# Modulation vectors by rows: GpSimd multiplies, ScalarE sums

## Chip, cores and metric

The kernel runs on one core of a Trainium2 chip. The metric is the device time of one execution in microseconds (us), as the median of several runs. A core has the engines TensorE (PE in the profile, its weight loads apart as PEld), VectorE (DVE), ScalarE (ACT), GpSimd (POOL) and SyncE (SP), which here only issues DMAs. Each runs its own list of instructions in order, and they meet by semaphores.

## What is computed

Two blocks of two layers each, on 256 tokens of width 1024, all in float32. Every layer derives shift, scale and gate, 3072 numbers, from a condition vector and a matrix of 1024 x 3072. The second block does it for two conditions (the tokens' and the context's).

```python
c_silu = jax.nn.silu(c)                                  # first block, one condition
mod = c_silu @ w_ada + b_ada
shift, scale, gate = jnp.split(mod, 3, axis=-1)
u = rms_norm(x, norm_g) * (1 + scale[:, None]) + shift[:, None]
z = u @ w_in                                             # then three attentions, gates, w_out
...
shift, scale, gate = jnp.split(jax.nn.silu(c) @ w_ada + b_ada, 3, axis=-1)       # second block
shift_c, scale_c, gate_c = jnp.split(jax.nn.silu(c_ctx) @ w_ada + b_ada, 3, axis=-1)
```

The rest of a layer is a wide projection, several attentions (one with a search for the top 64 keys of each query, one with a sliding window and sinks, one "stick-breaking"), gates and an output projection.

## The kernel before

The work is written as five scripts, one for each stage: prologue (the first modulation of layer 0), one0 and one1 (the two layers of the first block, one1 with the context's part of the second block's first layer), two0 and two1 (the second block). A script is a list of items such as ("proj", "cq", 0, (0,)) or ("logits", 3). Every engine walks the same list and emits its own instructions for each item, so the script sets the order on all five, and an engine that waits at an item holds up all of its later items.

Names of items: "proj" is a projection of 256 output columns, 16 products of 128x128 by 128x256 on TensorE and a copy out of PSUM on ScalarE (on VectorE for av, bv, cv). A job is one piece of attention: "logits" (TensorE, then a maximum on VectorE and exponentials on ScalarE), "soft" (VectorE scales them), "turn" (TensorE transposes, ScalarE copies), "mix" (TensorE by the values, VectorE copies). In stick-breaking jobs GpSimd masks in "soft" and "turn". weave() puts a projection between these steps so that TensorE has work while a chain runs. "rot" is the rotary embedding (VectorE shuffles and multiplies, GpSimd multiplies by the cosine and adds, L2260 and L2268). "dots" is the score of the key search, and pick_keys its search on VectorE (L2167 to L2185). "merge" adds a branch, "out" is the output projection, "stats" and "start" make the normalised input u. In the prologue the first four projections ("lead") run ahead, and "take" copies them out on ScalarE.

Weights come through a ring of five slots of 1 MB. A unit (an item of UNIT_KINDS) uses one slot, in order. SyncE walks the units: it waits until a unit is used up (L849 to L855) and then asks for the unit five places on. The results of projections go through three PSUM banks, in turn: full says that TensorE has written one, drained that it has been copied out.

The modulation is made in three ways:

- "mve" in the prologue and "mva" elsewhere (L927): TensorE multiplies the condition, held as 32 columns of weights, by 256 columns of the matrix, 8 products each; two of them make a group of 512. VectorE copies the strips of the result (L1705); "ada" transposes them on TensorE (L941), and VectorE adds them up with the bias (L1740, L1743). one1 does so for the last group of w1 (its own gate) and for the six groups of v0 (the second block, layer 0).
- "mvd" in one0, for the gate of w0 and groups 0 to 4 of w1: VectorE multiplies four blocks of rows of the matrix by the condition's numbers and adds them up (L1715, L1717), and "col" sums over the partitions on TensorE (L948, with a matrix of ones).

```python
at = heavy(s)
s = modulate_on_vector(s, [at[7 + 9 * n // 2:] for n in range(len(groups))], (0, 2, 4), groups)
...
s = modulate(s, heavy(s)[2::4][:6], 2, [("v0", g) for g in range(6)])
s[1:1] = group("w1", 5)
```

heavy() lists the places of the projections, merges and output projections. The first group of one1 stands right behind "start".

## Time and profile before

| | |
|---|---|
| median of 3 runs | 1434.23 us (1433.36 to 1435.22) |
| span of the profiled execution (the page gives no other time of it) | 1434.8 us |
| TensorE busy | 1391.2 us |
| VectorE, ScalarE, GpSimd busy | 609.2, 414.1, 164.8 us |
| granted TensorE clock, mean | 0.995 |
| read from HBM | 221.04 MB, 155 GB/s |
| stages (us from the start) | prologue to 57.6, one0 to 391.7, one1 to 879, two0 and two1 to 1434.8 |

A row of a timeline gives the start, the duration, the engine, the line of the kernel, the operation and what it writes and reads; in brackets the idle time of the engine before it and what ended it. Each product in float32 appears twice in the records, so a projection's 16 are "x32". The spans on GpSimd are rough.

### The profile page before, as it was taken

The page shows a single profiled execution, that of the slowest core. Times are in us where ns is not written, and L with a number is a line of the kernel's source. Part 1 is how long each engine was busy: PE and PEld are TensorE (multiplying, and loading weights), DVE is VectorE, ACT ScalarE, POOL GpSimd, SP SyncE. Part 2 cuts the span into 40 slices and gives each one's busy share as a digit, 9 for nine tenths or more (in the row PEclk, how much of TensorE's full clock was granted, in tenths as well). Part 3 has the DMA queues.
Part 4 walks back from the last instruction along what each step waited for, and adds up shares of the span by engine and source line. Part 5 has one row for each costly group of instructions (what it writes and reads, how often), then busy time and mean ns, then how long its engine had stood idle before and what let it go on. Part 6 is the DMA issues. An engine that isn't in the chain of part 4 may idle for free.

```text
span 1434.8 us, 19837 instructions
## 1 busy us (share of the span) xinstructions
PE 1391.2 (97%) x7898; PEld 1141.3 (80%) x7898; DVE 609.2 (42%) x1377; ACT 414.1 (29%) x769; POOL 164.8 (11%) x191
## 2 busy tenths in 40 slices
PE   6999999999999999999999999999999999999996
PEld 4878888888878888888888878877777788877764
DVE  1465334233236442323235441155584532467466
ACT  2122222311021222333323211332244422433442
POOL 0201200000011030000112100013140000233000
PEclk9999999999999999999999999999999999999999
DMA  9534455465464444443333332445322333432230
GB/s 372 214 124 155 180 205 181 157 240 208 163 249 176 177 176 176 169 167 119 145 118 134 125 124 88 147 155 224 151 89 89 118 120 142 180 118 89 89 147 30
DMA packets 31629, 223.38 MB, mean 156 GB/s; under 512 B 3889, under 2 KB 4017, under 8 KB 4913
## 3 DMA queue, kind: packets, MB, share of 16 engines
q1 hardware_dynamic: 31536, 222.11, 42.1%
q8 instruction: 63, 1.03, 0.3%
q14 instruction: 30, 0.24, 0.0%
HBM read 221.04 MB, written 1.05 MB: 155 GB/s over the span
## 4 chain that ended last, share of the span: by engine, by line
PE 88%; DVE 7%; ACT 2%; issue 2%; POOL 1%; DMA 1%; DVEq 0%; SPq 0%; ACTq 0%; POOLq 0%
PE event L992 44%; PE event L983 9%; PE event L1136 6%; PE event L1202 5%; PE logits L1068 3%; PE mixed_out L1124 3%; PE turns L1087 3%; PE event L927 2%; PE event L1229 2%; PE event L1161 1%; PE event L1166 1%; PE logits L959 1%; PE event L1302 1%; PE event L971 1%; DVE logits L1810 1%
## 5 line engine op out<-in xcount | busy, mean ns | idle before, releaser
L992 PE MATMUL event<-u,ring 128*128 128x256 f32 x3072 | 684.2, 381 | 2.9 <-DVE region L2132 1.7
L992 PEld LDWEIGHTS event<-u,ring 128*128 128x128 f32 x3072 | 577.0, 190 | 95.6 <-issue 17.0
L983 PE MATMUL event<-ring,u 128*128 128x256 f32 (+1 forms) x704 | 151.6, 372 | 0.0
L983 PEld LDWEIGHTS event<-ring,u 128*128 128x128 f32 x704 | 127.9, 191 | 21.7 <-issue 5.6
L2260 POOL TENSOR_TENSOR raw<-raw,tables 128x512 f32<-128x512 f32 (+1 forms) x28 | 44.6, 1593 | 727.2 <-DVE turned L1786 538.8
L1429 ACT ACTIVATE S<-logits,stat 128x512 f32<-128x512 f32 (+2 forms) x160 | 83.9, 535 | 133.6 <-DVE stat L1825 124.2
L1393 ACT ACTIVATE region<-event 128x512 f32<-128x512 f32 x72 | 43.0, 597 | 275.0 <-PE event L992 274.8
L1202 PE MATMUL event<-region,ring 128*128 128x256 f32 x384 | 85.4, 380 | 3.3 <-DVE region L1968 3.3
L1202 PEld LDWEIGHTS event<-region,ring 128*128 128x128 f32 x384 | 72.1, 190 | 15.8 <-issue 6.5
L1136 PE MATMUL event<-region,ring 128*128 128x256 f32 x384 | 84.4, 380 | 0.0
L1136 PEld LDWEIGHTS event<-region,ring 128*128 128x128 f32 x384 | 72.6, 190 | 10.7 <-issue 1.0
L1445 ACT ACTIVATE PT<-turns 128x1024 f32<-128x1024 f32 (+1 forms) x52 | 44.7, 860 | 82.3 <-PE turns L1087 81.9
L1068 PE MATMUL logits<-region 64*128 64x256 f32 (+4 forms) x320 | 60.8, 482 | 4.5 <-ACT S L1429 3.0
L1802 DVE TENSOR_REDUCE stat<-logits 128x2 f32<-128x1024 f32 (+1 forms) x32 | 39.2, 1224 | 53.8 <-PE logits L1068 53.1
L1124 PE MATMUL mixed_out<-PT,region 128*64 128x128 f32 (+2 forms) x584 | 55.2, 298 | 2.2 <-ACT PT L1445 2.0
L2132 DVE COPY_PREDICATED region<-tables,event 128x512 f32<-128x512 uint32 x42 | 30.9, 735 | 58.5 <-PE event L1229 57.4
L1124 PEld LDWEIGHTS mixed_out<-PT,region 128*64 128x64 f32 x584 | 38.7, 138 | 17.3 <-issue 12.7
L1884 DVE COPY region<-mixed_out 128x256 f32<-128x256 f32 (+3 forms) x60 | 21.7, 362 | 67.9 <-PE mixed_out L1124 57.6
L1087 PE MATMUL turns<-consts,S 128*128 128x128 f32 x336 | 47.9, 281 | 0.0
L1087 PEld LDWEIGHTS turns<-consts,S 128*128 128x128 f32 x336 | 36.1, 141 | 11.2 <-issue 9.8
L2234 POOL TENSOR_TENSOR region<-region 128x256 f32<-128x256 f32 x24 | 16.0, 668 | 249.0 <-PE event L1229 154.6
L1068 PEld LDWEIGHTS logits<-region 64*128 64x128 f32 (+1 forms) x320 | 24.7, 188 | 22.7 <-issue 15.9
(242 smaller groups left out, 1365.9 us busy)
## 6 DMA issues: line engine op xcount, KB each, us to landing
ring<-in_w SPq DMA_DIRECT2D x196, 1024.0 KB, 4.9
region<-in_quick SPq DMA_DIRECT2D x8, 1024.0 KB, 18.8
region<-in_rows SPq DMA_DIRECT2D x1, 1536.0 KB, 8.1
tables<-in_two SPq DMA_DIRECT2D x1, 1472.0 KB, 9.1
x<-in_x SPq DMA_DIRECT2D x1, 1024.0 KB, 7.4
x<-in_ctx SPq DMA_DIRECT2D x1, 1024.0 KB, 6.7
out<-x SPq DMA_DIRECT2D x4, 256.0 KB, 2.3
tables<-in_one SPq DMA_DIRECT2D x1, 768.0 KB, 29.3
```

The costliest lines, as they stand in the source:

```text
L983: ins = mm(bank[:, t * 256:t * 256 + width], mem.u[:, q, k, t * P:(t + 1) * P], wt[:, k * 256:k * 256 + width], start=k == 0, stop=k == KB ...
L992: ins = mm(bank[:, j * 256:(j + 1) * 256], wt[:, k * 256 + j * P:k * 256 + j * P + P], mem.u[:, q, k, :], start=k == 0, stop=k == KB - 1)
L1068: ins = mm(out, q, k, start=True, stop=True)
L1087: ins = eng.transpose(mem.TR[:, i * P:(i + 1) * P], S[:, at:at + P], c["ident"])
L1124: ins = mm(out, value_of(mem, job, m, kt), turned[:, :, kt, :], start=kt == 0, stop=kt == tiles - 1)
L1136: ins = mm(bank[:, j * 256:(j + 1) * 256], wt[:, at:at + P], mem.one["y"][:, 4 * br + k, :], start=k == 0, stop=k == 3)
L1202: ins = mm(bank[:, j * 256:(j + 1) * 256], wt[:, at:at + P], src[:, k, :], start=k == 0, stop=k == KB - 1)
L1393: act(dst, split2(bank), func, scale=scale).then_inc(drained[e % BANKS], 1)
L1429: ins = act(S[:, m * K:(m + 1) * K], mem.LG[:, m * K:(m + 1) * K], ACT.Exp, bias=stat[:, 1, m:m + 1], accum_out=stat[:, 2, m:m + 1])
L1445: act(mem.PT[:, n % 2, 0:cols], mem.TR[:, 0:cols], ACT.Copy).then_inc(sems["turns_copied"], 1)
L1802: eng.tensor_reduce(stat[:, 0, 0:nm], mem.LG[:, 0:nm * K].rearrange("p (m k) -> p m k", m=nm), AX.X, ALU.max).then_inc(mine, 1)
L2260: tt(shape(mem.raw), shape(mem.raw), wide(cosine, width // T), ALU.mult).then_inc(mine, 1)
```

## The change

"mva", "ada", "mvd" and "col" disappear from one0 and one1. The matrix is now laid out by its output columns: a unit "mvr" brings 256 of them, one on each partition and twice 128, with their 1024 input numbers along the row. GpSimd multiplies 128x1024 of them by the condition's row, which stands on every partition, into one of two scratch tiles ("multiplied"). ScalarE copies the scratch tile onto itself and lets the accumulator sum along the row straight into the modulation tile ("summed"). The first half of a unit is the item "mvr", the second "mvs". For v0 each half is done for both conditions. A last step "bias" on VectorE adds the bias once for each tag; it waits for all of the tag's sums. GpSimd may be two products ahead of ScalarE, since it waits for the sum before the last one.

In one0 there are now 20 such units (w0 8 to 11, w1 0 to 7, v0 0 to 7), in one1 eight (w1 8 to 11, v0 8 to 11); before there were 14 of mvd in one0 and 14 of mva in one1. Their halves are spread evenly over the places of heavy(). The bias of w1's gate comes right ahead of ("logits", 0) in one1. The new item "rows" in one0 applies Silu to the condition's rows on ScalarE; it stands behind proj("bv"), ahead of ("take", 2). SyncE asks for these rows (0.5 and 1 MB) right behind the first refill of the ring. The step that feeds the context's u moves behind ("logits", 4), and three small loads for the second block come at unit 12 instead of 20.

```diff
-    groups = [("w0", 4), ("w0", 5)] + [("w1", g) for g in range(5)]
-    at = heavy(s)
-    s = modulate_on_vector(s, [at[7 + 9 * n // 2:] for n in range(len(groups))], (0, 2, 4), groups)
+    s = modulate_by_rows(s, heavy(s)[3:-5], units_of("w0", 4, 5) + units_of("w1", 0, 1, 2, 3) + units_of("v0", 0, 1, 2, 3))
...
-    s = modulate(s, heavy(s)[2::4][:6], 2, [("v0", g) for g in range(6)])
-    n = s.index(("ada", 3, "v0")) + 1
+    at = heavy(s)
+    n = s.index(("logits", 4)) + 1
     s[n:n] = [("mod", "v0"), ("feed", 1, "v0")]
-    s[1:1] = group("w1", 5)
-    s.insert(s.index(proj("iq")) + 1, ("ada", 5, "w1"))
+    s = modulate_by_rows(s, at[2:13], units_of("w1", 4, 5) + units_of("v0", 4, 5))
...
+def modulate_by_rows(s, at, units):
+    halves = []
+    for n, (tag, i) in enumerate(units):
+        halves.append([("mvr", i, tag)])
+        halves.append([("mvs", i, tag)])
+        own = [j for t, j in units if t == tag]
+        if i == own[-1]:
+            halves[-1].append(("bias", tag, 2 * own[0], 2 * own[-1] + 2))
...
+        if n in at:
+            k = at.index(n)
+            for items in halves[k * len(halves) // len(at):(k + 1) * len(halves) // len(at)]:
+                out += items
...
# SyncE
-                elif item[0] == "mvd":
+                elif item[0] == "mvr":
                     eng.wait_ge(sems["worked"], w.at("worked", sec.index(item) + 1))
...
+            if item == ("lead", 0):
+                eng.dma_start(mem.cond_row, dram["cond_row"]).then_inc(sems["cond_row_in"], 16)
+                eng.dma_start(mem.cond_rows, dram["cond_rows"]).then_inc(sems["cond_rows_in"], 16)
...
# ScalarE
+            elif kind in ("mvr", "mvs"):
+                i, tag, b = item[1], item[2], int(kind == "mvs")
+                conds = conds_of(tag, i)
+                for n in range(conds):
+                    k = sec.sums_through(item) - conds + n
+                    eng.wait_ge(sems["multiplied"], w.at("multiplied", k + 1))
+                    act(mem.scratch[:, k % 2], mem.scratch[:, k % 2], ACT.Copy,
+                        accum_out=mem.mods[tag][:, 2 * i + b, n:n + 1]).then_inc(sems["summed"], 1)
+                    eng.wait_ge(sems["summed"], w.at("summed", k + 1))
...
+            elif kind == "rows":
+                eng.wait_ge(sems["cond_row_in"], 16)
+                act(mem.cond_row, mem.cond_row, ACT.Silu)
+                eng.wait_ge(sems["cond_rows_in"], 16)
+                act(mem.cond_rows, mem.cond_rows, ACT.Silu).then_inc(sems["rows_ready"], 1)
+                eng.wait_ge(sems["rows_ready"], w.at("rows_ready", 1))
+                exps()
...
# VectorE
+            elif kind == "bias":
+                eng.wait_ge(sems["summed"], w.at("summed", sec.sums_through(last)))
+                tt(mods, mods, biases.unsqueeze(2).broadcast_to([P, b - a, conds]), ALU.add).then_inc(mine, 1)
...
# GpSimd
+                part, conds = mem.ring[:, row % RING, D * b:D * b + D], conds_of(tag, i)
+                for n in range(conds):
+                    k = sec.sums_through(item) - conds + n
+                    times = mem.cond_row if tag[0] == "w" else mem.cond_rows[:, n]
+                    if k >= 2 or sec.name != "one0":
+                        eng.wait_ge(sems["summed"], w.at("summed", k - 1))
+                    tt(mem.scratch[:, k % 2], part, times, ALU.mult).then_inc(sems["multiplied"], 1)
+                    eng.wait_ge(sems["multiplied"], w.at("multiplied", k + 1))
```

How this stands in the engines' lists is shown at the start of one1. First GpSimd, at the ropes of that stage (raw and turned are the rope's tiles). Before, from the last mask of one0 on:

```order
L2204 AFFINE_SELECT PT<-PT 128x4x128 x2
L2260 TENSOR_TENSOR raw<-raw,tables 128x512
L2268 TENSOR_TENSOR region<-raw,turned 128x512
L2260 TENSOR_TENSOR raw<-raw,tables 128x512
L2268 TENSOR_TENSOR region<-raw,turned 128x512
```

And now, from the second half of w1's unit 8 to unit 11, with the third and fourth rope (L2280, L2288) of the stage between them:

```order
L2303 TENSOR_TENSOR region<-ring,region 128x1024
L2306 MEMSET credit 128x1
L2303 TENSOR_TENSOR region<-ring,region 128x1024 x2
L2306 MEMSET credit 128x1
L2280 TENSOR_TENSOR raw<-raw,tables 128x512
L2288 TENSOR_TENSOR region<-raw,turned 128x512
L2303 TENSOR_TENSOR region<-ring,region 128x1024
L2280 TENSOR_TENSOR raw<-raw,tables 128x512
L2288 TENSOR_TENSOR region<-raw,turned 128x512
L2303 TENSOR_TENSOR region<-ring,region 128x1024
L2306 MEMSET credit 128x1
L2303 TENSOR_TENSOR region<-ring,region 128x1024 x2
```

Before, ropes followed each other; now three products stand ahead of the third rope, one between it and the fourth, and three behind the fourth.

ScalarE, at the same place before, from the first "dots" (L1407) to the exponentials of job 0 (L1429):

```order
L1407 ACTIVATE PT<-logits 128x2x256
L1390 ACTIVATE raw<-event 128x512
L1407 ACTIVATE PT<-logits 128x1024
L1393 ACTIVATE region<-event 128x512 x3
L1427 ACTIVATE stat<-stat 128x8
L1429 ACTIVATE S,stat<-logits,stat 128x128 x8
```

And now, where L1439 is "dots", L1358 the sum and L1461 the exponentials:

```order
L1439 ACTIVATE PT<-logits 128x2x256
L1422 ACTIVATE raw<-event 128x512
L1358 ACTIVATE region,mod_w<-region 128x1024 x2
L1439 ACTIVATE PT<-logits 128x1024
L1425 ACTIVATE region<-event 128x512
L1358 ACTIVATE region,mod_w<-region 128x1024
L1425 ACTIVATE region<-event 128x512
L1358 ACTIVATE region,mod_w<-region 128x1024 x2
L1425 ACTIVATE region<-event 128x512
L1358 ACTIVATE region,mod_w<-region 128x1024
L1459 ACTIVATE stat<-stat 128x8
L1461 ACTIVATE S,stat<-logits,stat 128x128 x8
```

Six sums now stand between the first "dots" and the exponentials of job 0. In VectorE's list the end of the second search, the last rope and the maxima of job 0 (L1830) now have the bias (L1749) between them:

```order
L2205 SCALAR_TENSOR_TENSOR region<-region,tables 128x256
L1806 STREAM_SHUFFLE turned<-raw 128x512
L1810 TENSOR_TENSOR turned<-turned,tables 128x512
L1749 TENSOR_TENSOR mod_w<-mod_w,par 128x8
L1830 ISA logits,stat<-logits,tables 128x128
```

Before, a copy of the strips stood there:

```order
L2185 SCALAR_TENSOR_TENSOR region<-region,tables 128x256
L1786 STREAM_SHUFFLE turned<-raw 128x512
L1790 TENSOR_TENSOR turned<-turned,tables 128x512
L1705 COPY strips<-event 128x512
L1810 ISA logits,stat<-logits,tables 128x128
```

The copy waited for TensorE's group of v0; the bias waits for all of w1's sums.

## Rows read from the trace of the kernel before

**Rows 1.** Page, part 1: busy us, share and instructions of each engine

```profile
PE 1391.2 (97%) x7898; PEld 1141.3 (80%) x7898; DVE 609.2 (42%) x1377; ACT 414.1 (29%) x769; POOL 164.8 (11%) x191
```

**Rows 2.** Windows, stages one0 and one1: length, busy of PE, PEld, DVE, ACT, POOL

```profile
57.60:391.70 334.10, 328.49 (x1680) 281.30 (x1679) 134.83 (x312) 72.33 (x134) 25.16 (x22) 0.99 0.49 181
391.70:879.00 487.30, 482.87 (x2768) 400.39 (x2766) 181.57 (x461) 134.26 (x266) 54.17 (x58) 1.00 0.43 157
```

**Rows 3.** Timeline, PE: start, duration, operation, idle before it and its releaser

```profile
98.51 2.08 PE L1068 MATMUL logits<-region 64*128 64x256 f32 x8 [2.75 <-ACT S L1429]
362.95 14.05 PE L1202 MATMUL event<-region,ring 128*128 128x256 f32 x64 [1.67 <-DVE region L1968]
397.52 7.85 PE L992 MATMUL event<-u,ring 128*128 128x256 f32 x32 [0.49 <-ACT u L1339]
466.39 1.13 PE L1068 MATMUL logits<-region 64*128 64x256 f32 x8 [0.29 <-ACT S L1429]
```

**Rows 4.** Critical chain, one "col", one group of "mva", one "ada": start, duration

```profile
158.01 0.79 PE event L948 x8
448.54 1.86 PE event L927 x32
405.37 0.44 PE event L941 x4
```

**Rows 5.** Windows of lines L948, L927, L941 alone: busy (records) of PE, PEld

```profile
57.60:391.70 334.10, 6.64 (x56) 7.35 (x56) 0.99 0.49 181
391.70:879.00 487.30, 13.54 (x224) 6.56 (x224) 1.00 0.43 157
391.70:879.00 487.30, 4.37 (x28) 3.26 (x28) 1.00 0.43 157
```

**Rows 6.** Timeline, VectorE and GpSimd at a rope, and VectorE with GpSimd idle

```profile
63.01 1.71 POOL L2260 TENSOR_TENSOR raw<-raw,tables 128x512 f32<-128x512 f32 x1 [3.96 <-DVE turned L1786]
63.63 1.12 DVE L2167 TENSOR_SCALAR small<-region 128x4 f32<-128x4 f32 x1
64.78 1.44 DVE L2171 SCALAR_TENSOR_TENSOR region<-PT,small,tables 128x128 f32<-128x128 f32 x1
64.80 1.27 POOL L2268 TENSOR_TENSOR region<-raw,turned 128x512 f32<-128x512 f32 x1
...
427.19 0.17 DVE L2167 TENSOR_SCALAR small<-region 128x4 f32<-128x4 f32 x1 [0.95 <-ACT PT L1407]
```

**Rows 7.** Groups by line and shape: count, busy us, mean ns, idle before

```profile
L2236 POOL TENSOR_TENSOR region<-region 128x256 f32<-128x256 f32 x24 | 15.7, 653 | 1.9
L1485 ACT ACTIVATE region<-region 128x1024 f32<-128x1024 f32 x28 | 29.6, 1057 | 6.9 <-POOL region L2240 6.1
L1429 ACT ACTIVATION_READ_ACCUMULATOR S<-logits,stat 128x1 f32 x160 | 32.3, 202 | 0.0
L1454 ACT ACTIVATE region<-region 128x2048 f32<-128x2048 f32 x6 | 11.5, 1910 | 0.1
L1317 ACT ACT_TABLE_LOAD x20 | 25.7, 1283 | 0.4
```

**Rows 8.** Page, part 6: KB, us to landing; and SyncE's timeline, first refill

```profile
region<-in_rows SPq DMA_DIRECT2D x1, 1536.0 KB, 8.1
...
50.81 3.78 SPq L857 DMA_DIRECT2D ring<-in_w  x2
```

**Rows 9.** Critical chain, "take 2" of one0 on ScalarE

```profile
61.38 0.61 ACT raw L1346
```

**Rows 10.** Timeline, one1: the last rope on GpSimd and logits 0 on TensorE

```profile
455.13 1.26 POOL L2268 TENSOR_TENSOR region<-raw,turned 128x512 f32<-128x512 f32 x1
457.44 1.16 PE L1068 MATMUL logits<-region 64*128 64x128 f32 x16
```

**Rows 11.** Timeline, one0's last drain on ScalarE and last merge on VectorE

```profile
332.86 0.60 ACT L1393 ACTIVATE region<-event 128x512 f32<-128x512 f32 x1 [6.31 <-PE event L992]
...
362.11 0.69 DVE L1968 TENSOR_TENSOR region<-region 128x512 f32<-128x512 f32 x1
```

More of the change, by code:

```diff
@@ L98 @@
 LEAD = [("iq", 0), ("ik", 0), ("bq", 0), ("bq", 1)]
-UNIT_KINDS = ("mva", "mvd", "lead", "proj", "merge", "out", "outa", "outb")
+UNIT_KINDS = ("mva", "mvr", "lead", "proj", "merge", "out", "outa", "outb")
 EARLY, LATE = (0, 1, 2, 3, 6, 7), (4, 5)
@@ L174, in modulate_on_vector, with units_of, conds_of @@
         out.append(item)
[L175 to L182 removed]
+        if n in at:
+            k = at.index(n)
+            for items in halves[k * len(halves) // len(at):(k + 1) * len(halves) // len(at)]:
+                out += items
+    return out
+def units_of(tag, *groups):
+    return [(tag, 2 * g + h) for g in groups for h in range(2)]
+def conds_of(tag, i):
+    return 1 if tag[0] == "w" else CONDS
 def proj(name, q=0, i=0):
@@ L386, in __init__ @@
         n["cond_ready"] = kinds.count("cond") + (name == "prologue")
-        n["worked"] = kinds.count("mvd")
+        n["worked"] = kinds.count("mvs")
+        n["multiplied"] = n["summed"] = sum(conds_of(i[2], i[1]) for i in script if i[0] in ("mvr", "mvs"))
+        n["rows_ready"] = kinds.count("rows")
         n["rs_ready"] = kinds.count("stats")
@@ L413, in events @@
             return item[1] % 2
-        return {"proj": 1, "out": 1, "ada": 1, "stats": 1, "outa": 1, "outb": 4, "col": 1, "row": 1, "flip": 1, "merge": 2, "norm": 1, "level": 2, "khatT": 2, "state": 1,
+        return {"proj": 1, "out": 1, "ada": 1, "stats": 1, "outa": 1, "outb": 4, "row": 1, "flip": 1, "merge": 2, "norm": 1, "level": 2, "khatT": 2, "state": 1,
                 "hout": 1, "mean": 1, "var": 1}.get(kind, 0)
@@ L445, in readers, with sums_through @@
         return [e, e + 1]
+    def sums_through(self, item):
+        return sum(conds_of(i[2], i[1]) for i in self.script[:self.script.index(item) + 1] if i[0] in ("mvr", "mvs"))
     def index(self, item):
@@ L909, in body @@
                 wt = mem.ring[:, slot, :]
-                if 0 in halves and kind != "mvd":
+                if 0 in halves and kind != "mvr":
                     eng.wait_ge(sems[f"landed{slot}"], 16 * (row // RING + 1))
@@ L941, in body @@
                     ins = eng.transpose(bank[:, b * P:(b + 1) * P], mem.strips[:, b * P:(b + 1) * P], c["ident"])
-                ins.then_inc(full[e % BANKS], 1)
-            elif kind == "col":
-                eng.wait_ge(sems["worked"], w.at("worked", 2 * sec.index(item) + 2))
-                eng.wait_ge(drained[e % BANKS], w.fills(e - BANKS))
-                for b in range(4):
-                    ins = mm(mem.bank[e % BANKS][:, CONDS * b:CONDS * b + CONDS], mem.strips[:, b * P:(b + 1) * P], c["ones"][:, 0:CONDS],
-                             start=b == 0, stop=b == 3, skip_group_check=True)
                 ins.then_inc(full[e % BANKS], 1)
```

74 lines of the change are left out of this document (31 added, 43 removed).

## Prediction

> **What bounds the kernel now.** I read the page's busy shares first, then the busy time by stage, then where TensorE sat idle, then the chain. The span is 1434.8 us; the page shows no other time of that execution, and the median of the three runs is 1434.23, so I add my sum to the median. TensorE is busy for 97% of the span [rows 1]. Stage one0 (57.6 to 391.7 us) leaves it 5.6 us of idle time, stage one1 (391.7 to 879) 4.4 us [rows 2]. So what TensorE no longer does in these stages is gained, unless a wait takes its place, and what delays another engine costs only where TensorE is waiting or nearly so. The idle rows name those places [rows 3]: at 98.51 it waited 2.75 us for the exponentials of job 0, which stand behind VectorE's search for the top keys; at 362.95 it waited 1.67 us for VectorE's last merge; at 397.52 for the first of u; at 466.39 for job 0's exponentials again. At 250 or 320 us nothing waits: there the chain of a softmax has several us to spare.
>
> **What goes.** In one0 seven "col" steps: one lasts 0.79 us on the chain, and 56 records are seven of 8 [rows 4, 5]. 7 x 0.79 = 5.5 us. In one1 seven groups of modulation at 1.86 us and seven "ada" steps at 0.44 us (224 records of 32, 28 of 4) [rows 4, 5]: 13.0 and 3.1 us. The first group stands where TensorE waits for u anyway: nothing is gained by it. Two "ada", two groups and the "ada" behind logits 0 lie before logits 1 of one1, where another chain decides (below); they count there. Left are 4 groups and 4 "ada", 9.2 us. VectorE also loses the "mvd" steps, but TensorE hardly waits for VectorE in the middle of one0, so I count that as nothing; its cover is TensorE's own 7 us projections.
>
> **What a multiply and a sum cost.** The trace has no GpSimd product of 128x1024. From below it is bounded by the 128x512 one, 1.27 us [rows 6]; 128x256 takes 0.65 [rows 7], so 256 columns more cost 0.61 and 1024 columns 1.27 + 2 x 0.61 = 2.5 us, which I take. From above: 3.4, twice the 1.71 of one that first waits for VectorE. The sum on ScalarE is 1.06 for 128x1024 plus some 0.1 to 0.2 for reading the accumulator [rows 7]: 1.2 us. The Trainium skill (GPSIMD Engine Reference, "3.1 Elementwise") gives 4497 ns for 2048 columns, which makes an estimate of 2.25 us for half; no run here shows it, and with it the result would be some 1.5 us lower. There are 80 products (16 units of w0 and w1 in two halves, 12 of v0 in two halves for two conditions: 32 + 48) and 80 sums: 200 us of GpSimd, 96 of ScalarE, in stages of 820 us, so neither is the bound by its total.
>
> **The port.** GpSimd's products hold up VectorE. At 63.01 GpSimd's rope product runs to 64.72; a TENSOR_SCALAR on 128x4 beside it takes 1.12 us and ends with it, against 0.17 at 427.19 when GpSimd is idle; the next VectorE instruction takes 1.44, again to about GpSimd's end [rows 6]. So a VectorE instruction of this kind that comes on a product waits up to 2.5 us. The Trainium skill (SBUF — State Buffer, "Who interferes with whom") says that the second of the two blocks fully; the rows agree. It also says that a VectorE instruction with one SBUF input outside the two-port modes isn't held up, which would spare MAX8 and MATCH_REPLACE8; no row here has one beside a product. I count them as free, with 2.5 us more as the bound.
>
> **one0, start.** ScalarE's new "rows" step stands ahead of "take 2", which began at 61.38 as soon as its data were there [rows 9]. It needs 1.5 MB that SyncE asks for right behind the refill of 50.81, by about 51.3; the 1.5 MB of in_rows took 8.1 us to land [rows 8], so the last is there at about 60. Then Silu on 128x2048 (1.91 [rows 7]) and a table load (1.28) end at 63.5 (the first load and the first Silu fit before): 2.1 us late, between 0 (data by 57) and 5. VectorE's top-key search starts as much later. At the second search GpSimd, done with the last rope, runs two products of w0 back to back (the row has landed, and only the third product waits for a sum). They meet the four scalar-tensor-tensors at the search's start: two of these wait, 2.2 + 2.1 = 4.3 us (0 to 5). TensorE already waits at the end of this chain, so the 6.4 us are paid in full at 98.51.
>
> **one0, middle.** Each softmax chain has some 7 us to spare and each stick-breaking one (VectorE, ScalarE, GpSimd between two TensorE steps 7 us apart) some 4; one product of 2.5 fits. 0 us, with 10 as the upper bound.
>
> **one0, merges.** The v0 part has 32 products of 2.5 = 80 us in 13 TensorE units of 6.9 = 90 us, and its bias waits for the last sum on VectorE ahead of the last merge. From the end of the last projection (ScalarE's drain at 332.86 [rows 11]): two sums left from mvs 5 and the "sig" step (1.28 + 1.91 + 1.28) occupy ScalarE to +10.6; GpSimd is then two products ahead, and six more at 2.5 go one after the other with the sums: +11.8 + 15 = +26.8, the sum +28.0, with waits for the port at VectorE's merges some +29.3. The last merge's four VectorE instructions (0.7 each) then end at +32.1. Today the last of them ends at 362.81 [rows 11], or +30.2 from 332.6, of which 0.8 is a col step that is gone: 29.4. So TensorE loses 2.7 us (0 to 5).
>
> **one1, start.** TensorE gets to logits 0 of this stage 4.6 us earlier (before 457.44 [rows 10]), but has to wait for the last rope, which ends on GpSimd at 456.4 now [rows 10]. ScalarE's sum ahead of "dots 0" leaves 1 us of TensorE's lead; products then meet the first search (about 1.6 us more) and the second (2.5 less what the rope already cost, 2.1 more): the rope ends at about 459. Now the new wait: behind it in GpSimd's order stand three products (mvs 10, mvr 11, mvs 11), each waiting for a sum two back, 7.6 us in all; the last sum 1.2; and VectorE has w1's bias ahead of logits 0, so its eight maxima (4.5 us, with the small ones) start only then, at 468, and ScalarE's exponentials (3.1) after them. logits 1 starts at 475.8 instead of 466.39: +9.4 us, the removed steps there included. Bounds: with no port waits and a short product (2.25) the rope ends at 455.4 and the row 5.7 later than now; with all waits, 12. Queued behind ScalarE's wait is the drain of "ck", but its bank is needed only two projections later, and SyncE's refills behind mvr 10 land some 10 us before "cv" needs them: nothing.
>
> **Sum.** -5.5 - 9.2 + 2.1 + 4.3 + 2.7 + 9.4 = +3.8 us: 1438.6 for the span, **1438.0** for the median. TensorE's later stages keep their order: 0.
>
> **Rivals.** (a) *TensorE's time wins.* GpSimd loses the fight for the port, the new rows come in time and the merge's bias is early: of the added terms only the serial part in one1 is left, 5.7 us. -5.5 - 9.2 + 5.7 = -9.0: 1425. For it: the 97% and the exact 14.7 us; against it: the row at 63.63, where VectorE lost. Chance 0.2. (b) *The softmax chains overflow.* Place: stick-breaking and softmax jobs of both stages; price: one more product (2.5) each beyond the 4 us to spare, which two products in a row (5 us) would reach; it decides if the sums on ScalarE come in bursts ahead of its exponentials. In four jobs +10: 1448. For it: ScalarE now stands waiting for GpSimd in program order; against it: TensorE has hardly a wait there today [rows 3]. Chance 0.2. (c) *The ring starves.* SyncE waits in order for "worked" of a row, holding back the refills behind it; if one row stays two projections longer, each such place costs about 5 us (a landing of 1 MB at the rate of the 1.5 in 8.1 [rows 8]): 1443. Chance 0.05. Left for the forecast, waits slightly larger than the work taken out: 0.55.
>
> **Chances.** About 0.2% (2.9 us) is what a measurement can tell. Faster, below 1431.3, is most of (a) and a little of the forecast's low end: 0.2. Within 0.2% is the lower third of the forecast and the upper end of (a): 0.25. Slower 0.55. The forecast's own range, from its terms' bounds partly used, is 1432 to 1445; to hold 8 in 10 it goes down to (a) and up to (b): 1425 to 1450.
>
> **What would show it.** In the changed profile: GpSimd products of 128x1024 at 2.2 to 2.8 us, 80 of them; no "col"; TensorE idle for 2.4 us at one1's first projection, where the group was; idle for about 9 us before logits 1 of one0; in one1 two idles, some 6 us before logits 0 and some 8 us before logits 1, released by GpSimd's rope and ScalarE's exponentials, with VectorE's bias waiting for ScalarE; VectorE instructions of 2 us in the searches; an idle of some 4 us before the first "out" of one0. TensorE's busy time should fall by about 19 us. The forecast is wrong if products take 1.3 us, if VectorE's instructions keep their length beside them, or if idle appears in the middle of the stages.

## The result and the profile after

The changed kernel takes 1.0045 times as long as the one before (95% interval 1.0032 to 1.0058): 1441.41 us against 1434.08 as medians of four runs each, some 6.5 us more by the ratio (4.6 to 8.3). The profiled execution has a span of 1440.1 us. The forecast was slower, 1438.0 in 1425 to 1450.

The page of the kernel after, part 1:

```profile
PE 1374.9 (95%) x7590; PEld 1130.6 (79%) x7590; DVE 599.1 (42%) x1298; ACT 512.0 (36%) x933; POOL 356.6 (25%) x299
```

TensorE is busy for 16.3 us less than in [rows 1], ScalarE for 98 us more and GpSimd for 192 more. The windows of the stages one0 and one1, cut at the same times as in [rows 2]:

```profile
57.60:391.70 334.10, 320.62 (x1604) 272.43 (x1604) 110.59 (x251) 140.65 (x249) 158.02 (x97) 0.98 0.54 202
391.70:879.00 487.30, 470.64 (x2477) 395.56 (x2476) 194.03 (x438) 158.22 (x308) 111.54 (x90) 0.98 0.39 142
```

TensorE's idle is 13.5 and 16.7 us now, against 5.6 and 4.4, and the mean granted clock fell from 0.99 and 1.00 to 0.98. The groups by shape show what a product and a sum cost (count, busy us, mean ns of one, idle before):

```profile
L2303 POOL TENSOR_TENSOR region<-ring,u 128x1024 f32<-128x1024 f32 x48 | 114.4, 2384 | 42.3 <-ACT region L1358 39.6
L2303 POOL TENSOR_TENSOR region<-ring,region 128x1024 f32<-128x1024 f32 x32 | 75.5, 2359 | 58.6 <-ACT region L1358 56.8
L1358 ACT ACTIVATE region<-region 128x1024 f32<-128x1024 f32 x80 | 84.7, 1058 | 57.9 <-POOL region L2303 56.4
L1358 ACT ACTIVATION_READ_ACCUMULATOR region<-region 128x1 f32 x80 | 15.0, 187 | 0.0
```

2.36 to 2.38 us for a product (2.5 assumed) and 1.2 for a sum. TensorE's waits, from its timeline; they answer to [rows 3]:

```profile
102.57 2.08 PE L1084 MATMUL logits<-region 64*128 64x256 f32 x8 [7.92 <-ACT S L1461]
365.10 29.55 PE L1218 MATMUL event<-region,ring 128*128 128x256 f32 x128 [4.36 <-DVE region L1988]
400.46 15.61 PE L1008 MATMUL event<-u,ring 128*128 128x256 f32 x64 [2.35 <-ACT u L1365]
462.20 2.08 PE L1084 MATMUL logits<-region 64*128 64x128 f32 x16 [5.90 <-POOL region L2288]
479.94 2.08 PE L1084 MATMUL logits<-region 64*128 64x256 f32 x8 [6.47 <-ACT S L1461]
```

Their brackets say 7.92, 4.36, 2.35, 5.90 and 6.47 us: 27.0 together, where the kernel before had 2.75, 1.67, 0.49, nothing and 0.29, that is 5.2. The places and releasers are those of the forecast. At 260 us the wait is 1.20 us in both. But two things stand in these rows that the prediction has not: job 1's logits take 2.08 us and not 1.13 as in the last of [rows 3], and so do job 0's in one1 (1.16 before [rows 10]). The windows of TensorE say why. First the kernel after (length, busy and records, granted clock, DMA share, GB/s):

```profile
100.00:104.00 4.00, 1.43 (x6) 0.50 0.01 2
104.00:108.00 4.00, 4.00 (x15) 0.67 0.00 0
...
364.00:368.00 4.00, 2.90 (x9) 0.76 0.83 350
...
400.00:404.00 4.00, 3.54 (x9) 0.57 0.00 0
...
464.00:468.00 4.00, 4.00 (x13) 0.50 0.53 174
...
480.00:484.00 4.00, 4.00 (x13) 0.50 0.00 0
```

Then the kernel before:

```profile
96.00:100.00 4.00, 1.49 (x8) 0.79 0.74 262
...
876.00:880.00 4.00, 3.87 (x44) 0.57 0.20 82
```

Behind each of the five waits the granted clock stands at the lower of its two levels (0.50, 1.2 GHz) for some us, and 4 us hold 13 records of TensorE's products where they hold 20 at the higher. Before, this happened once in these stages for less time (behind the wait at 98 us), and once at 876. I call it a dip.

**How the traces are laid side by side.** The first copy of a lead on ScalarE ("take 0") starts between 48.8 and 51.5 us in the traces of this study, for kernels whose prologue is the same, and all that follows moves with it. Here before and after:

```profile
50.87 0.60 ACT L1346 ACTIVATE raw<-logits 128x512 f32<-128x512 f32 x1 [2.56 <-PE logits L959]
```

```profile
49.76 0.60 ACT L1372 ACTIVATE raw<-logits 128x512 f32<-128x512 f32 x1 [2.56 <-PE logits L975]
```

So I subtract it. One dip more, worth some 1.6 us, falls somewhere between 870 and 1010 us in six of the thirteen traces (before, e1_bias_late, e2_one1_late, e5_warm, e7_best, e8_tuned); the trace of before has it at 876, that of after has none. A trace is one execution, so that it is missing in one doesn't belong to the kernel. So I compare up to one1's first "out" after TensorE's long wait there, and not at the end. In us behind take 0 (one1 from "iq" on; the last column is that "out"):

| kernel | one0 logits 1 | one0 out | iq | one1 logits 1 | one1 out |
|---|---|---|---|---|---|
| before | 47.6 | 312.1 | 346.7 | 415.5 | 788.7 |
| after | 52.8 | 315.3 | 350.7 | 430.2 | 796.7 |
| e6_split | 52.8 | 313.0 | 346.7 | 416.1 | 789.3 |
| e1_bias_late | 52.8 | 315.7 | 351.7 | 425.7 | 791.1 |
| e2_one1_late | 53.0 | 315.8 | 351.7 | 416.4 | 801.8 |
| e3_one0_start | 49.8 | 320.5 | 355.6 | 434.3 | 800.6 |
| e4_one0_end | 52.9 | 314.7 | 348.4 | 427.0 | 793.3 |
| e5_warm | 52.8 | 315.0 | 348.7 | 427.3 | 793.5 |
| e5b_warm_full | 52.9 | 313.4 | 347.1 | 425.8 | 789.5 |
| e7_best | 49.7 | 314.9 | 348.6 | 416.6 | 782.0 |
| e8_tuned | 47.6 | 308.6 | 342.2 | 410.2 | 774.2 |
| e8_tuned_warm | 47.6 | 305.6 | 339.2 | 407.2 | 771.2 |
| e9_before_warm | 47.6 | 310.5 | 345.1 | 414.0 | 787.2 |

**one0, start.** Timelines of ScalarE, GpSimd and VectorE, kernel after:

```profile
61.51 0.60 ACT L1372 ACTIVATE raw<-turns 128x512 f32<-128x512 f32 x1
...
79.14 4.91 POOL L2303 TENSOR_TENSOR region<-ring,region 128x1024 f32<-128x1024 f32 x2
79.38 5.47 DVE L2191 SCALAR_TENSOR_TENSOR region<-PT,small,region 128x256 f32<-128x256 f32 x3
...
88.50 2.35 POOL L2303 TENSOR_TENSOR region<-ring,region 128x1024 f32<-128x1024 f32 x1 [4.29 <-ACT region L1358]
89.44 0.43 DVE L2196 MAX8 small<-region 128x8 f32<-128x256 f32 x1
```

Take 2 comes 11.75 us behind take 0, against 10.51: the rows cost 1.24 us. The three scalar-tensor-tensors take 5.47 us beside two products, where they take 1.53 in the second search of the kernel before: 3.94 us. Together 5.2, and that is how much later logits 1 starts (52.8 for 47.6). MAX8 keeps its 0.43 us beside a product, as at 89.44. The rule of the Trainium skill (SBUF — State Buffer, "Who interferes with whom") that the prediction weighed is borne out on both sides: instructions with two SBUF inputs wait, MAX8 with one does not. No row names the mode of an instruction, so the rule's exception for the two-port modes can't be read here.

**one0, end.** ScalarE's last sum of v0, the bias behind it, and the last merge instruction:

```profile
360.62 1.06 ACT L1358 ACTIVATE region<-region 128x1024 f32<-128x1024 f32 x1 [1.29 <-POOL region L2303]
361.86 0.19 DVE L1749 TENSOR_TENSOR mod_v<-mod_v,par 128x32 f32<-128x32 f32 x1 [5.99 <-ACT region L1358]
...
364.26 0.69 DVE L1988 TENSOR_TENSOR region<-region 128x512 f32<-128x512 f32 x1
```

VectorE waited 5.99 us for that sum with both halves of the last merge behind it.

**one1, start.** The rope, the products, the last sum, the bias and the exponentials:

```profile
460.80 1.26 POOL L2288 TENSOR_TENSOR region<-raw,turned 128x512 f32<-128x512 f32 x1
462.14 2.35 POOL L2303 TENSOR_TENSOR region<-ring,region 128x1024 f32<-128x1024 f32 x1
464.73 4.78 POOL L2303 TENSOR_TENSOR region<-ring,region 128x1024 f32<-128x1024 f32 x2
469.59 1.06 ACT L1358 ACTIVATE region<-region 128x1024 f32<-128x1024 f32 x1 [0.37 <-POOL region L2303]
470.85 1.27 DVE L1749 TENSOR_TENSOR mod_w<-mod_w,par 128x8 f32<-128x8 f32 x1 [11.25 <-ACT region L1358]
...
476.88 0.21 ACT L1459 ACTIVATE stat<-stat 128x8 f32<-128x8 f32 x1 [6.14 <-DVE stat L1845]
```

The rope ends at 462.06, three products follow one after another to 469.5, the last sum is out at about 470.8, the bias comes then (and itself waits out a product: 1.27 us, where the larger one of v0 took 0.19), and only behind it VectorE's maxima and ScalarE's exponentials.

### The profile page after: what moved, and what is told of

The parts are those of the page before. It is cut to its first block, busy times and chain, and to the rows that moved or that the text cites. A ratio compares the mean times of both kernels' runs of the same rounds, so it can differ in the third digit from the quotient of the medians.

```text
span 1440.1 us, 19551 instructions
## 1 busy us (share of the span) xinstructions
PE 1374.9 (95%) x7590; PEld 1130.6 (79%) x7590; DVE 599.1 (42%) x1298; ACT 512.0 (36%) x933; POOL 356.6 (25%) x299
## 4 chain that ended last, share of the span: by engine, by line
PE 82%; DVE 9%; POOL 3%; issue 3%; ACT 2%; DMA 0%; DVEq 0%; SPq 0%; ACTq 0%; POOLq 0%
PE event L1008 41%; PE event L999 9%; PE event L1218 5%; PE event L1152 4%; PE logits L1084 3%; PE mixed_out L1140 3%; PE turns L1103 3%; POOL region L2303 2%; PE event L1245 2%; PE event L1177 1%; PE event L1182 1%; DVE region L2191 1%; PE logits L975 1%; DVE region L2199 1%; PE event L1318 1%
## 5 line engine op out<-in xcount | busy, mean ns | idle before, releaser
L2280 POOL TENSOR_TENSOR raw<-raw,tables 128x512 f32<-128x512 f32 (+1 forms) x28 | 43.2, 1543 | 463.1 <-DVE turned L1806 412.6
L1461 ACT ACTIVATE S<-logits,stat 128x512 f32<-128x512 f32 (+2 forms) x160 | 83.9, 536 | 127.8 <-DVE stat L1845 123.1
L2303 POOL TENSOR_TENSOR region<-ring,u 128x1024 f32<-128x1024 f32 x48 | 114.4, 2384 | 42.3 <-ACT region L1358 39.6
L1358 ACT ACTIVATE region<-region 128x1024 f32<-128x1024 f32 x80 | 84.7, 1058 | 57.9 <-POOL region L2303 56.4
L2303 POOL TENSOR_TENSOR region<-ring,region 128x1024 f32<-128x1024 f32 x32 | 75.5, 2359 | 58.6 <-ACT region L1358 56.8
```

The lines of the kernel that those rows point to most:

```text
L1358: act(mem.scratch[:, k % 2], mem.scratch[:, k % 2], ACT.Copy, accum_out=mem.mods[tag][:, 2 * i + b, n:n + 1]).then_inc(sems["summed"], 1)
L1461: ins = act(S[:, m * K:(m + 1) * K], mem.LG[:, m * K:(m + 1) * K], ACT.Exp, bias=stat[:, 1, m:m + 1], accum_out=stat[:, 2, m:m + 1])
L2280: tt(shape(mem.raw), shape(mem.raw), wide(cosine, width // T), ALU.mult).then_inc(mine, 1)
L2303: tt(mem.scratch[:, k % 2], part, times, ALU.mult).then_inc(sems["multiplied"], 1)
```

## The experiments

Medians and ratios to the kernel before, which ran again beside each group of experiments (medians 1434.17, 1434.38 and 1435.58 us), with 95% intervals:

| kernel | median us | ratio |
|---|---|---|
| e1_bias_late | 1437.83 | 1.0021 (1.0009 to 1.0033) |
| e2_one1_late | 1448.25 | 1.0092 (1.0077 to 1.0107) |
| e3_one0_start | 1447.53 | 1.0090 (1.0072 to 1.0107) |
| e4_one0_end | 1439.23 | 1.0041 (1.0027 to 1.0056) |
| e5_warm | 1439.37 | 1.0028 (1.0016 to 1.0039) |
| e5b_warm_full | 1436.09 | 1.0008 (0.9998 to 1.0017) |
| e6_split | 1434.47 | 0.9992 (0.9980 to 1.0004) |
| e7_best | 1429.34 | 0.9961 (0.9946 to 0.9976) |
| e8_tuned | 1418.81 | 0.9880 (0.9865 to 0.9896) |
| e8_tuned_warm | 1416.41 | 0.9866 (0.9853 to 0.9879) |
| e9_before_warm | 1433.30 | 0.9986 (0.9977 to 0.9995) |

**1. The change in one0 alone.**

```diff
-    s = modulate_by_rows(s, heavy(s)[3:-5], units_of("w0", 4, 5) + units_of("w1", 0, 1, 2, 3) + units_of("v0", 0, 1, 2, 3))
+    s = modulate_by_rows(s, heavy(s)[3:-5], units_of("w0", 4, 5) + units_of("w1", 0, 1, 2, 3, 4))
...
-    s = modulate_by_rows(s, at[2:13], units_of("w1", 4, 5) + units_of("v0", 4, 5))
+    s = modulate(s, heavy(s)[2::4][:6], 2, [("v0", g) for g in range(6)])
+    s[1:1] = group("w1", 5)
...
```

> The change in one0 alone: w0's gate and groups 0 to 4 of w1 by rows (28 products, none of v0 in the merges), and one1 as in the kernel before, with TensorE making w1's group 5 and all of v0. Theory: seven cols less (-5.5), rows late by 1.2 and the second search by 3.9 (+5.2 before logits 1), about +1 to 1.5 for the longer dip of the clock, nothing in the merges: +0.5 to +1.5 us against the kernel before, 1435. So most of the loss of the whole change comes from the merges' v0 part and from one1. Rival (one0's start is the whole loss and one1 breaks even): 1439 or more. Rival (the rows in the middle of one0 cost nothing and the cols are a clean gain): 1429.

TensorE's waits in its trace, at logits 1 of one0 and at iq:

```profile
104.28 2.08 PE L1085 MATMUL logits<-region 64*128 64x256 f32 x8 [7.89 <-ACT S L1462]
...
398.18 8.04 PE L1009 MATMUL event<-u,ring 128*128 128x256 f32 x32 [0.49 <-ACT u L1366]
```

The loss of 5.2 us at the start is whole, iq stands where it stood, so the seven cols pay for the start and its longer dip; one1's out is 0.6 us later than before. As expected. The loss of the whole change lies in v0's part of the merges and in one1.

**2. The bias moved.** It goes from ahead of logits 0 to behind soft 1.

```diff
+    b = next(i for i in s if i[0] == "bias" and i[1] == "w1")
+    s.remove(b)
+    s.insert(s.index(("soft", 1)) + 1, b)
```

> Only w1's bias is moved on VectorE, from ahead of logits 0 of one1 to behind soft 1. Theory (three serial products and sums hold ScalarE, and the bias holds VectorE's maxima behind them): the last of the three sums still ends about 8.5 us after logits 0 began, but the eight maxima (4.5 us with their small ones) now run beside it, and the exponentials (3.1 us) start right behind the sum. The wait before logits 1 falls from 6.47 to about 1 us and its start comes some 5.5 us earlier; the whole falls from 1440.1 to about 1434.5. Rival (the bias is only a witness and something else holds the maxima or the exponentials): no change. Rival (ScalarE alone holds the row): no change either, since the exponentials would be no earlier.

VectorE, ScalarE and TensorE in its trace:

```profile
467.54 1.22 DVE L1844 TENSOR_TENSOR stat<-stat,par 128x8 f32<-128x8 f32 x1
469.00 2.37 DVE L1848 TENSOR_SCALAR stat<-stat 128x8 f32<-128x8 f32 x1
471.48 0.21 ACT L1462 ACTIVATE stat<-stat 128x8 f32<-128x8 f32 x1 [1.49 <-DVE stat L1848]
...
474.54 1.56 PE L1087 MATMUL logits<-region 64*128 64x256 f32 x8 [3.23 <-ACT S L1464]
```

The maxima now run beside the sums, and logits 1 starts 4.5 us earlier behind take 0 (5.5 expected). What is missing of it stands in the rows: a tensor-scalar of 128x8, 0.17 us when GpSimd is idle, takes 2.37 beside a product, and a tensor-tensor of the same size 1.22. The whole fell by 0.24% of the time before (3.4 us), the distance to one1's out by 5.6 us, some of which is the dip behind the shorter wait of 3.23 us. Both rivals fall.

**3. one1's units behind logits 0.**

```diff
-    s = modulate_by_rows(s, at[2:13], units_of("w1", 4, 5) + units_of("v0", 4, 5))
+    s = modulate_by_rows(s, at[8:15], units_of("w1", 4, 5) + units_of("v0", 4, 5))
```

> All of one1's units go to the seven places from proj ck 1 on, behind logits 0; nothing of them is left in the two key searches, the ropes or ahead of the exponentials of job 0. Theory: the last rope ends relative to one1's start as in the kernel before (456.4 - 391.7 = 64.7 us), logits 0 waits some 3 to 4 us because TensorE has less work ahead of it, logits 1 comes at about the old distance, 8.9 us after logits 0, and the pair of clock dips (a stretch at 0.5 of the granted clock behind each wait of about 6 us) is reduced to one or none: -10 us for the start of logits 1, -2 for the clock, but 24 products of 2.4 us now lie in some 58 us of TensorE's time, so up to +5 by waits in jobs 1 to 4: 1428 to 1433. Rival (the start of one1 is set by something else, such as the new loads): above 1438.

The start does what was expected: logits 1 stands 13.8 us earlier (the waits there are 0.76 and 0.66 us), 0.9 us behind the kernel before. But the time is 1448, and here is where it went, from the timelines of TensorE, GpSimd, ScalarE and VectorE:

```profile
521.85 1.22 PE L1046 MATMUL turns<-region 64*128 64x256 f32 x4 [6.24 <-ACT PT L1477]
...
528.08 9.67 POOL L2303 TENSOR_TENSOR region<-ring,u 128x1024 f32<-128x1024 f32 x4
537.85 1.06 ACT L1358 ACTIVATE region<-region 128x1024 f32<-128x1024 f32 x1 [1.28 <-POOL region L2303]
539.09 0.17 DVE L1749 TENSOR_TENSOR mod_v<-mod_v,par 128x16 f32<-128x16 f32 x1 [27.17 <-ACT region L1358]
552.38 1.22 PE L1046 MATMUL logits<-region 64*128 64x256 f32 x4 [10.53 <-POOL PT L2224]
```

GpSimd goes from products to ropes and back without a gap until 537.8, ScalarE stands in between waiting for each, VectorE waits 27.17 us for the bias, and the stick-breaking jobs, which need all three, hold TensorE for 6.24 and 10.53 us. I had priced this at up to 5 us; it cost 18.8 (385.3 us from logits 1 to out against 366.5). It is rival (b)'s mechanism, brought about by density.

**4. one0's start moved.**

```diff
-    s = modulate_by_rows(s, heavy(s)[3:-5], ...
+    s = modulate_by_rows(s, heavy(s)[7:-5], ...
...
-    s = [..., proj("bv"), ("rows",), ("rest", 2), ...
-         ..., ("dots", 1), proj("cq"), ...
+    s = [..., proj("bv"), ("rest", 2), ...
+         ..., ("dots", 1), ("rows",), proj("cq"), ...
```

> Two moves at the start of one0: the rows step on ScalarE stands behind dots 1 instead of ahead of take 2, and the first unit behind aq 0 (the eighth place) instead of behind ck 0, so that its weights land after VectorE's second search. Theory: take 2 comes 1.2 us earlier against take 0, the three scalar-tensor-tensors of the second search take 1.5 us instead of 5.5, so the wait before logits 1 of one0 is 2.75 us as in the kernel before instead of 7.92, and the dip of the clock behind it is as short as before (some 1 us less). Logits 1 starts 47.6 us behind take 0 (52.8 in the changed kernel). The 56 products now lie in 29 places instead of 33; if that overflows the stick-breaking jobs, up to +5 there. Without that: -6 us, 1434.5. Rival (the search is slow for another reason than the product beside it): the wait stays above 6 us.

```profile
92.71 4.79 POOL L2303 TENSOR_TENSOR region<-ring,region 128x1024 f32<-128x1024 f32 x2 [13.79 <-issue]
...
95.33 2.20 DVE L1845 TENSOR_SCALAR stat<-stat 128x8 f32<-128x8 f32 x1
...
371.33 29.36 PE L1218 MATMUL event<-region,ring 128*128 128x256 f32 x128 [8.40 <-DVE region L1988]
```

A miss: 6 us less were expected, 6 more than the changed kernel were measured. The search is free of products and take 2 on time, but the first two products now start at 92.71, when their weights land, and catch the small tensor-scalar on which job 0's exponentials wait: 2.20 us instead of 0.17. So the wait is 4.95 and not 2.75. And the loss is at the other end, which I had not counted: the same products in fewer places, with the same last one, put v0's last sum later still (its end lies 317.1 us behind take 0, against 312.0), and the first out waits 8.40 us instead of 4.36. Two small waits came as well, 2.12 us instead of 1.20 for the last turn's copy at 261.76, with a dip behind it, and 1.33 for weights at 341.94.

**5. one0's end moved.**

```diff
-    s = modulate_by_rows(s, heavy(s)[3:-5], ...
+    s = modulate_by_rows(s, heavy(s)[3:-9], ...
```

> The places of one0 end four earlier, so v0's last sum comes some 28 us before the last merge; the start is untouched. Theory: the bias no longer holds VectorE's last merge, the wait before the first out falls from 4.36 to the 1.67 of the kernel before, and with it goes the dip of the clock in the first out (the 128 products of 128x256 take 27.9 us as in the split kernel, not 29.6): -2.7 and -1.5, and less in the start of one1, together -4 to -5 us, 1436. Rival (the wait before out has another cause): 4.36 stays. Rival (the denser middle overflows the stick-breaking jobs): waits of some us appear between 150 and 230 us.

The wait before out is 1.67 us, its 128 products take 27.86 us, and iq comes 2.3 us earlier; out itself only 0.6, because a "mix" at 265 us waits 2.92 us instead of 1.20: two sums stand ahead of the last turn's copy on ScalarE, and no work of TensorE lies between. 3.3 us less at one1's out, of 4 to 5 expected; the medians cannot tell it from the changed kernel. So the cause at the end is the bias, and what the denser middle takes back shows at 265 us and not between 150 and 230.

**6. TensorE kept busy in its waits.** Nothing is moved; products whose result nobody reads are put ahead of the waits.

```diff
+    def warm(n):
+
+        for _ in range(n):
+            mm(mem.out[:, 0:T], c["ident"], mem.consts[:, 0:T], start=True, stop=True, skip_group_check=True)
...
         for item, e, u in w.items():
+            warm(WARM.get((sec.name,) + item[:2], 0))
```

> Nothing is moved. TensorE gets products of 128x128 by 256 columns whose result nobody reads, ahead of its five long waits: 14 before logits 1 of one0 (7.92 us of idle), 7 before the first out of one0 (4.36), 3 before iq of one1 (2.35), 10 before logits 0 (5.90) and 12 before logits 1 of one1 (6.47), each set shorter than the wait it stands in. Theory (the granted clock falls to half for some 4 us behind each of these waits, and TensorE's next work pays for it): the clock stays at 1.0 there, the first 16 products of a projection take 7.1 us instead of 9.3, each place gives back 1 to 3 us: together -5 to -8 us, about 1434. Rival (the clock in the records costs nothing, the waits alone do): no change, 1440.

Three of the five dips went (at out, iq and logits 0, where 1.35, 1.06 and 1.57 us of waiting were left), two stayed (1.87 and 4.30 us left). One1's out came 3.2 us earlier, less than expected, by the two that stayed. For iq this run proves little: e1 to e4 have the same wait of 2.35 us there without idle products, and none of them has a dip behind it.

> As the kernel with idle products of TensorE ahead of its five long waits, but with more of them (17, 9, 5, 13, 20 instead of 14, 7, 3, 10, 12), so that no wait of over about 1 us is left. There two dips of the clock were left, where 1.87 and 4.30 us of waiting remained. Theory: both vanish too (cv's first products at 7.1 us for 16 instead of over 8), logits 1 of both stages start when the exponentials are done, and the projection behind each gains 1.5 to 3 us: -3 to -5 against the first such kernel, 1434 to 1436, so that the dips are worth 6 to 8 us of the changed kernel's time. Rival (a dip comes from something other than the wait): the clock still shows 0.5 there and nothing is gained.

Windows of TensorE with the larger numbers; those of after for the same stretches stand above:

```profile
104.00:108.00 4.00, 4.00 (x24) 1.00 0.00 0
...
480.00:484.00 4.00, 4.00 (x20) 1.00 0.00 0
```

No dip is left in these stages, and one1's out stands 7.1 us earlier than in the changed kernel, 0.8 us behind the kernel before. The ratio falls from 1.0045 to 1.0008. All the waits for the other engines are still there; only TensorE's clock behind them is different. So the dips are worth some 7 us in the traces; by the ratios it is 5.3 us (0.37%, give or take 0.16). That is about the size of the whole loss, but the kernel before has a dip in these stages too, which experiment 7 prices.

**7. The same in the kernel before.**

> The kernel before with the same 6 idle products ahead of logits 1 of one0, where it waits 2.75 us and the clock shows 0.79 in the 8 us behind. Theory: the clock stays at 1.0 there, logits 1 takes 1.1 us instead of 2.1, and the whole is 1 to 1.5 us shorter (0.1%), whatever the way in which the modulation is made. Rival (dips belong to something that the change brought): no difference.

```profile
97.94 1.13 PE L1075 MATMUL logits<-region 64*128 64x256 f32 x8
```

Logits 1 takes 1.13 us instead of 2.08, iq comes 1.6 us earlier behind take 0, the ratio is 0.9986 (2.0 us). Dips are not the change's own; in its trace there are four more, and the one at logits 1 lasts longer there than before.

**8. A version that keeps what works.** One0 gets w0's gate, w1's groups 0 to 4 and v0's 0 to 2, with a number of products for each place; one1 gets v0's 4 and 5 behind logits 0; TensorE keeps w1's group 5 and v0's group 3 at the start of one1, where it waits anyway. Rows stand behind dots 1 as in experiment 4.

```diff
+ROOM = {7: 2, 8: 1, 9: 1, 10: 1, 11: 1, 12: 2, 13: 1, 14: 1, 15: 1, 16: 1, 17: 2, 18: 2, 19: 2, 20: 2, 21: 2, 22: 2, 23: 3, 24: 3, 25: 3, 26: 3, 27: 3, 28: 3, 29: 3, 30: 3, 31: 3, 32: 3}
...
-    s = modulate_by_rows(s, heavy(s)[3:-5], units_of("w0", 4, 5) + units_of("w1", 0, 1, 2, 3) + units_of("v0", 0, 1, 2, 3))
+    s = modulate_by_rows(s, {heavy(s)[k]: c for k, c in ROOM.items()}, units_of("w0", 4, 5) + units_of("w1", 0, 1, 2, 3, 4) + units_of("v0", 0, 1, 2))
...
-    s = modulate_by_rows(s, at[2:13], units_of("w1", 4, 5) + units_of("v0", 4, 5))
+    s = modulate_by_rows(s, at[8:13], units_of("v0", 4, 5))
+    s = modulate(s, heavy(s)[2:3], 2, [("v0", 3)])
+    s[1:1] = group("w1", 5)
+    s.insert(s.index(proj("iq")) + 1, ("ada", 5, "w1"))
...
```

> What the runs so far suggest: one0 by rows from its eighth place on with at most one product in a place between stick-breaking jobs, two between softmax jobs, three in the merges, and ended four places before the last merge; v0's groups 0 to 2 in one0 and 4 and 5 in one1 behind logits 0; TensorE keeps w1's group 5 and v0's group 3, both at the start of one1, where it has to wait for the rope anyway. Theory: seven cols (-5.5) and four groups with their adas behind logits 1 (-9.2) are gained, no new wait of over 2.5 us and no new dip of the clock: 1434.2 - 14.7 = 1419.5, between 1418 and 1424. Rival (the products overflow some chain wherever they are put): waits of 2 to 10 us between 120 and 250 us and between 500 and 560, 1428 or more.

```profile
99.98 2.08 PE L1097 MATMUL logits<-region 64*128 64x256 f32 x8 [4.83 <-ACT S L1474]
261.60 1.54 PE L1153 MATMUL mixed_out<-PT,region 128*64 128x128 f32 x16 [2.12 <-ACT PT L1490]
328.72 1.56 PE L1021 MATMUL event<-u,ring 128*128 128x256 f32 x6 [2.04 <-DMA ring<-in_w]
...
501.54 0.70 PE L1059 MATMUL logits<-region 64*128 64x256 f32 x4 [1.55 <-ACT PT L1490]
```

Faster than before, but 5 us above the expected range. The waits are small ones: the tensor-scalar of experiment 4 again; two sums ahead of the last turn's copy; at 328.72 a wait for weights, which is rival (c): v0's units occupy their ring slots for 9.7 us each, and the refills behind them come late; and at 501.54 one for ScalarE's copy of a turn.

> The mixed version moved by what its trace showed: first unit one place later (its products met the small tensor-scalar ahead of job 0's exponentials, 2.20 us instead of 0.17), no unit between m 3 and the gates of one0 (two sums stood ahead of the last turn's copy: 2.12 us of waiting and a dip of the clock), v0's products in one0 at 2.5 in a place instead of 3 and up to the fourth merge (a refill came 2.04 us late), and in one1 one half instead of two ahead of turn 1 (1.55 us). Theory: these waits go (-2.1, -0.9 and some 2 of the dip, -2.0, -1.5), nothing new comes: 8 us less than the mixed version, some 1420 to 1422. Rival (GpSimd has too much to do in one0 and each move only shifts the wait): 1427 to 1430.

The edit changes only the table of places and gives one1's five places 2, 4, 4, 2 and 4 products:

```diff
+ROOM = {8: 2, 9: 1, 10: 1, 11: 1, 12: 2, 13: 1, 14: 1, 15: 1, 16: 2, 17: 2, 18: 2, 19: 2, 20: 2, 21: 2, 23: 3, 24: 2, 25: 3, 26: 2, 27: 3, 28: 2, 29: 3, 30: 2, 31: 3, 32: 2, 33: 3, 34: 2}
```

```profile
98.43 2.08 PE L1097 MATMUL logits<-region 64*128 64x256 f32 x8 [2.71 <-ACT S L1474]
...
359.39 27.86 PE L1231 MATMUL event<-region,ring 128*128 128x256 f32 x128 [1.67 <-DVE region L2001]
...
461.04 1.14 PE L1097 MATMUL logits<-region 64*128 64x256 f32 x8 [1.02 <-ACT S L1474]
```

All four waits are back to what they are in the kernel before, or gone, and one1's out is 7.8 us earlier: ratio 0.9880, 17 us below the kernel before and a little below the expected range. Behind take 0 that out comes 14.5 us earlier than before, against 14.7 from cols, groups and adas in the prediction's first two terms. The traced execution is the slowest of the five.

> The same with 6 idle products of TensorE ahead of logits 1 of one0, some 2.7 us in a wait of 2.75. Theory: the dip of the clock behind that wait goes: 1 to 1.5 us less than without. Rival: no difference.

Out of one0 stands 3.0 us earlier behind take 0, twice what was expected, since the dip in e8_tuned was longer than that of the kernel before although its wait was as short (2.71 for 2.75 us; granted clock in 102 to 106 us 0.65, before 1.00). So the length of a wait doesn't fix what its dip costs. The ratio is 0.9866; the two intervals overlap, so the medians alone don't show the difference, but the trace has no dip there (logits 1 at 1.14 us). This is the best version run, 1.3% faster than the kernel before.

## Why the prediction was right, and where it was not

The sign, the places, the releasers and the mechanisms came out. Each term of the sum, in the traces:

| term | forecast | measured |
|---|---|---|
| cols | -5.5 | -6.0 |
| groups and adas behind logits 1 of one1 | -9.2 | -9.4 (363.8 us from logits 1 to out without dips in e5b_warm_full, 373.2 before) |
| rows ahead of take 2 | +2.1 | +1.2 |
| port at the second search of one0 | +4.3 | +3.9 |
| the merge's bias in one0 | +2.7 | +2.7 (4.36 for 1.67) |
| start of one1, iq to logits 1 | +9.4 | +9.8 without dips in e5b_warm_full, +10.6 with |
| softmax and stick-breaking chains | 0 | 0: no new wait in the middle of either stage |
| sum of these, to one1's out | +3.8 | +2.4 (789.5 in e5b_warm_full for 787.2 in e9_before_warm) |
| TensorE's clock behind waits | not in the sum | +5.6 (7.1 in the changed kernel, less 1.6 in the kernel before) |
| all, to one1's out | | +7.9 |

The cols show between e9_before_warm and e5b_warm_full, which have no dip in one0: from logits 1 to out 262.9 and 260.6 us, and of the latter 2.8 are more waiting ahead of out (0.47 and nine idle products of 0.44, against 1.67). So 5.1 us went there, with six of the seven cols, 4.7 by the forecast's 0.79 each; the seventh lies behind out, where 0.9 went up to iq.

The step that failed is the one that is missing: "TensorE's busy time should fall by about 19 us", and with it the price of a wait. I took a wait of TensorE to cost its own length. The pieces that the prediction takes out make 5.5 + 13.0 + 3.1 = 21.6 us, and how it came from there to 19 it doesn't say. Busy time fell by 16.3, since the work behind a wait ran at half the clock: 21.6 less the 5.6 of the table is 16.0. The prediction had the row of it, logits 1 at 98.51 with 2.08 us where the same eight products take 1.13 at 466.39 [rows 3], and did not read it.

With this term the sum closes: 2.4 and 5.6 make, but for rounding, the 7.9 us that the traces show at one1's out (796.66 for 788.72), and 7.9 lies within the 4.6 to 8.3 of the medians. The forecast's own terms came out 1.4 us too high, by the rows' 0.9, the port's 0.4 and the cols' 0.5, with 0.4 back at the start of one1. By the ratios the two parts are about equal: e5b_warm_full stands 0.22% (3.2 us) above e9_before_warm, and the rest is the clock. So half of the loss or more is a term that the prediction didn't have. That the total fell near 1438.0 was partly luck, and so is a loss clear of noise: what the prediction priced measured 2.4 us, less than the 2.9 that it says a measurement can tell.

The rivals: (a), TensorE's time wins, fell because GpSimd does not lose the fight for the port (5.47 against 1.53 us). (b), the chains overflow, did not happen in the change, but did as soon as the same products were laid more densely (e2_one1_late). (c), the ring starves, did not happen either, and appeared in e7_best for 2.04 us and in e3_one0_start for 1.33. So both named real limits on the other side of the schedule that was chosen. That 14.7 us of TensorE's time were there to be had, as (a) said, is shown by e8_tuned, with 14.5, and without dips on either side by e8_tuned_warm against e9_before_warm, with 16.0 (771.2 for 787.2). These versions leave two groups to TensorE at the start of one1; with that, the loss lay in the places of the products, not in the exchange of engines. Whether all 14 could go without a loss no run shows.

## What to carry to other kernels

Price a new wait of the busiest engine at more than its length where the profile shows its clock falling behind waits, and look for that in the rows at hand: the same instruction with two durations. When work is moved to engines that were idle, ask what stands next to each piece in their lists: three products and a bias at the wrong spot (+9.8 us) took back what the groups behind them gave (-9.4), and the same pieces all a few places on, but laid densely, cost 18.8 us elsewhere; only fewer pieces, spread, kept the gain. Spread such pieces by their cost, not by their number, and keep them off places where a chain has no cover.

## What was not expected of the hardware

- The dips: a wait of 4.3 us or more had one behind it every time; of the waits of 1.9 to 3.3 us some had (1.87 in e5_warm, 2.12 in e7_best, 2.35 at iq in the changed kernel, 2.75 before, 3.23 in e1_bias_late), some not (2.04 at 328.72 in e7_best, 2.35 at iq in e1 to e4, 2.92 in e4_one0_end). What decides it stays open. Products without use, 0.44 us each, kept the clock up.
- VectorE's tensor-scalar of 128x8 waits for GpSimd's product to its end (2.20 and 2.37 us instead of 0.17), as the one of 128x4 in [rows 6] did. It has one SBUF input, as MAX8 has, so the number of inputs alone doesn't decide. Job 0's maxima, with their logits in PSUM (0.30 us, at 92.73 to 93.74 in e7_best), and MAX8 (0.43) keep their length beside one.
- The eight scalings of job 0's probabilities in "soft" (tensor-scalar, 128x128) suffer the same way: 3.84 us in the changed kernel at 103.06, with a product at 104.47 beside them, against 1.66 before. Nothing waited for them there.
